# The recurrent layer of a three-layer transformer kernel: gates, first convolution tap, exponentials and b_o in another order

## The chip, the cores and the metric

The kernel runs on one core of one Trainium2 chip. The metric is the device time of one execution in microseconds (us), as the median of several executions.

## What is computed

A sequence of 256 tokens with 1024 channels, all in float32, passes two models one after the other. The first has an attention layer and a recurrent layer, each followed by a feed-forward layer with squared ReLU; the second has one layer with two gated feed-forward parts around a mixer of attention and pooling. The change concerns the recurrent layer alone:

```python
def rglru_block(h, w_in, b_in, conv_w, conv_b, w_ga, b_ga, w_gx, b_gx, a_param, w_o, b_o):
    u = jnp.einsum('bsd,de->bse', h, w_in) + b_in
    x_br = u[..., :D_RNN]
    y_br = jax.nn.gelu(u[..., D_RNN:], approximate=True)
    xp = jnp.pad(x_br, ((0, 0), (CONV_WIDTH - 1, 0), (0, 0)))
    xc = conv_b + xp[:, 0:S] * conv_w[0]
    for tap in range(1, CONV_WIDTH):
        xc = xc + xp[:, tap:tap + S] * conv_w[tap]
    xb = xc.reshape(B, S, N_RG_BLOCKS, RG_BLOCK)
    r = jax.nn.sigmoid(einsum('bsnc,nce->bsne', xb, w_ga) + b_ga)
    ig = jax.nn.sigmoid(einsum('bsnc,nce->bsne', xb, w_gx) + b_gx)
    log_a = -RG_C * r * jax.nn.softplus(-a_param)
    a = jnp.exp(log_a)
    mult = jnp.sqrt(-jnp.expm1(2.0 * log_a))
    b_seq = mult * (ig * xc)
    hs = scan of h = a * h + b_seq over the tokens
    return jnp.einsum('bse,ed->bsd', hs * y_br, w_o) + b_o
```

Here S is 256 and D_RNN is 1024, which the kernel keeps as eight blocks of 128 channels (one block fills the 128 partitions); a gate is a product of a block with its own 128 by 128 matrix.

## The kernel before

**Weights.** All weights pass through TensorE in 167 pieces of 1 MB (128 partitions x 2048 values), in one fixed order. SyncE loads piece n into one of six `raw` buffers, and may do so once piece n - 6 has been split. ScalarE (ACT) copies it to `w_hi`, rounded to fp32r (`hi(n)`, line 318), which needs one of three buffers and so waits until piece n - 3 has been used. VectorE (DVE) subtracts that from the raw piece (`lo(n)`, line 586). A product in full precision is then three fp32r matmuls: high by high, high by low, low by high. The activations are split in the same way into `xT_hi` and `xT_lo`. TensorE waits for both halves of a piece in `split(n)`.

**Order.** Each engine runs a program written out by hand, strictly in its order; they meet in semaphores. Whatever stands behind a waiting instruction on an engine waits too.

**The recurrent layer.** Pieces 48 to 55 (N_REC = 48) are the columns of `w_in`, two channel blocks each: 48 to 51 give the x branch, 52 to 55 the y branch. A piece is eight blocks of six matmuls (`u_block`, lines 1206 to 1209) into one PSUM bank. Pieces 56 to 59 (N_RO = 56) are the rows of the output matrix, 24 matmuls of 512 columns each (`d_part`, line 1230); the last two are closed in an order of their own (`closing`), and FM1, the next feed-forward layer, begins with piece 60.

For a pair p of channel blocks (2p and 2p + 1) the steps are these:

- `x_pair(p)` on VectorE (line 894) takes the pair out of PSUM, times the tokens' rms factor.
- The first tap with the bias is done by GpSimd (POOL, line 1133), the other three taps of both blocks by VectorE in `conv(p)` (line 903), each waiting for the one before.
- `gates(n)` on TensorE (lines 1479 and 1480) needs all taps of block n. The gates of pair p are issued inside piece 50 + p, after its blocks 3 and 6.
- `gates(n)` on ACT takes two sigmoids (lines 478 and 481) and a tanh (line 483) of them; `bx(n)` on GpSimd (line 1138) multiplies the input gate into the block.
- When all eight tanhs are done, ACT takes eight exponentials (line 505). GpSimd squares each (line 1152) into one of two buffers `sq`, VectorE turns square and tanh into the argument of the root (line 949), and ACT takes eight square roots (line 509).
- `scan(n)` on VectorE: for blocks 0 to 3 the product with the root (line 916), which GpSimd does for blocks 4 to 7 (line 1156), and the scan (line 920).
- `y_pair(p)` on VectorE (line 909) takes the y branch out of PSUM, ACT applies the gelu (line 488), `mixed(p)` on VectorE multiplies it with the scan (line 926), ACT copies the product to `xT_hi` (line 496), and VectorE forms `xT_lo` (line 929). The output products of piece 56 + p need both halves of pair p.

GpSimd then adds `b_o` to the residual `h`, in two additions of 128 x 1024 (line 1161), as soon as its own b products are done; VectorE waits for them (`h_bo`) before it adds the outputs to `h` in `turn(M1, ...)`. ACT changes its function tables on the way: the trace has an ACT_TABLE_LOAD ahead of the sigmoids, the exponentials, the roots and the gelus, one each.

VectorE's order in this stretch is: split of 50, rms factor, `x_pair(0)`; then for p = 0, 1, 2 the split of piece 51 + p, `conv(p)`, `x_pair(p + 1)`; split of 54, `conv(3)`, `y_pair(0)`, split of 55, the eight operations of line 949, `y_pair(1)`, split of 56, scans 0 and 1, `mixed(0)`, scans 2 to 7, split of 57, `y_pair(2)`, `mixed(1)`, `y_pair(3)`, `mixed(2)`, `mixed(3)`, splits of 58, 59 and 60.

Of the kernel before, what the change touches and what calls it, by code (L numbers as in the profile page):

```python
# [9 lines left out]
ACT = mybir.ActivationFunctionType  # L10
# [84 lines left out]
def build(nc, A, out):  # L95
# [217 lines left out]
    def scalar(e):  # L313
# [171 lines left out]
        def mixed(p):  # L485
            e.wait_ge(y_left, p + 1)
            for n in (2 * p, 2 * p + 1):
                e.activation(xb[:, n, 0:S], xb[:, n, 0:S], ACT.Gelu_apprx_tanh,
                             bias=col("b_in", KB + n)).then_inc(y_done, 1)
            for n in (2 * p, 2 * p + 1):  # L490
# [7 lines left out]
        for m in range(6):  # L498
            hi(N_REC + m + LOOK)
            if m >= 2:  # L500
                gates(2 * m - 4)
                gates(2 * m - 3)
        e.wait_ge(nt_done, KB)
        for n in range(KB):
            e.activation(rr[:, n, :], rr[:, n, :], ACT.Exp, scale=spn[:, n:n + 1]).then_inc(a_done, 1)
        hi(N_REC + 8)
        for n in range(KB):
            e.wait_ge(m_done, n + 1)
            e.activation(nt[:, n, :], nt[:, n, :], ACT.Sqrt).then_inc(mult_done, 1)
        mixed(0)  # L510
        hi(N_REC + 9)
        for p in range(1, 4):
            mixed(p)
        for n in (N_RO + 2, N_RO + 3, N_RO + 4):
            hi(n)
# [67 lines left out]
    def vector(e):  # L583
# [347 lines left out]

        e.wait_ge(ss_done, 4 * L1 + 4)
# [6 lines left out]
        for p in range(3):  # L939
            lo(N_REC + p + 3)  # L940
            conv(p)
            x_pair(p + 1)
        lo(N_REC + 6)
        conv(3)
        y_pair(0)
        lo(N_REC + 7)
        for n in range(KB):
            e.wait_ge(sq_done, n + 1)
            e.scalar_tensor_tensor(out=nt[:, n, :], in0=sq[n % 2], scalar=1.0, in1=nt[:, n, :], op0=ALU.add,  # L949
                                   op1=ALU.mult).then_inc(m_done, 1)  # L950
        y_pair(1)
        lo(N_REC + 8)
        scan(0)
        scan(1)
        mixed(0)
        for n in range(2, KB):
            scan(n)
        lo(N_REC + 9)
        y_pair(2)
        mixed(1)  # L960
        y_pair(3)
        mixed(2)
        mixed(3)
        for n in (N_RO + 2, N_RO + 3, N_RO + 4):
            lo(n)
# [131 lines left out]
    def gpsimd(e):  # L1097
# [32 lines left out]
        def conv(p):  # L1130
            e.wait_ge(x_left, p + 1)
            for n in (2 * p, 2 * p + 1):
                e.tensor_scalar(xc[:, n, :], xb[:, n, 0:S], col("conv_w", n), conv_bias[:, n:n + 1], ALU.mult,
                                ALU.add).then_inc(conv_first, 1)

# [3 lines left out]

        e.wait_ge(conv_pad, 1)  # L1140
        conv(0)
        for p in range(1, 4):
            conv(p)
            bx(2 * p - 2)
            bx(2 * p - 1)
        bx(6)
        bx(7)
        for n in range(KB):
            e.wait_ge(a_done, n + 1)
            if n >= 2:  # L1150
                e.wait_ge(m_done, n - 1)
            e.tensor_tensor(sq[n % 2], rr[:, n, :], rr[:, n, :], ALU.mult).then_inc(sq_done, 1)
# [6 lines left out]
        e.wait_ge(ss_done, 4 * L1 + 4)  # L1159
        for t in range(T):  # L1160
            e.tensor_tensor(h[:, t, :], h[:, t, :], bo, ALU.add).then_inc(h_bo, 1)
# [33 lines left out]
    def tensor(e):  # L1195
# [290 lines left out]
        for m in range(2, 6):  # L1486
            n, dst = N_REC + m, bank[[6, 4, 5, 6][m - 2]]
            if m >= 3:
                e.wait_ge(x_left, m - 2)
            split(n)  # L1490
            for k in range(KB):
                mm = u_block(n, k, dst)
                if k == KB - 1:
                    mm.then_inc(used, 1)
                if k == 3:
                    gates(2 * m - 4)
                if k == 6:
                    gates(2 * m - 3)
# [192 lines left out]
```

## Time and profile before

| | us |
|---|---|
| median of three executions | 1090.6 (1089.65 to 1091.54) |
| the profiled execution | 1087.43 |
| its span, from the first to the last instruction | 1085.6 |
| PE (TensorE matmul) busy in it | 1034.5 |
| PEld (weight load) busy | 951.8 |
| DVE (VectorE) busy | 684.7 |
| ACT (ScalarE) busy | 483.5 |
| POOL (GpSimd) busy | 91.4 |

The mean granted TensorE clock of the span is 0.985 of full speed. All times of a row count from the span's start. A busy PE is not PE at its peak: matmuls are pipelined, each record is longer than the step to the next one. The recurrent layer lies between about 325 and 412 us: piece 48 near 325, the output products from 388.84 on.

### The profile page before, as it was taken

To read this page: it belongs to the slowest core of one execution; us is meant where nothing else is said; L and a number is where in the kernel's file an instruction comes from. 1 tells how busy PE (TensorE), PEld (TensorE's weight loads), DVE (VectorE), ACT (ScalarE), POOL (GpSimd) and SP (SyncE) were. 2 spreads that over 40 slices of the span, in tenths; PEclk is the share of its full clock that TensorE was granted. 3 is DMA by queue.
4 is the path that set the end of the run, shared out by engine and by line. 5 is a ranking of instruction groups with operands and counts; after the bars stand their busy time and mean duration, and the time that the engine had idled before them with its cause. 6 is when DMAs were issued, how large, how long until landed. Compare 5 with 4: busy or idle time off the path is not lost.

```text
span 1085.6 us, 16423 instructions
## 1 busy us (share of the span) xinstructions
PE 1034.5 (95%) x6956; PEld 951.8 (88%) x6956; DVE 684.7 (63%) x835; ACT 483.5 (45%) x592; POOL 91.4 (8%) x88
## 2 busy tenths in 40 slices
PE   6999899999999959999999999999998789999997
PEld 5999799999989949999989999999987679999996
DVE  5577476655568797665565765565678645655565
ACT  5455353434345744434344644443444244344443
POOL 1200000000005621000000100000014300000000
PEclk9999999999999989999999999999999899999999
DMA  9943336555555325655556465645652226565511
GB/s 344 323 161 118 117 114 206 186 194 194 172 178 179 114 81 210 211 198 176 195 191 187 127 214 199 199 163 194 188 193 78 78 78 212 199 195 191 194 40 39
DMA packets 122838, 185.26 MB, mean 171 GB/s; under 512 B 3034, under 2 KB 102542, under 8 KB 122638
## 3 DMA queue, kind: packets, MB, share of 16 engines
q1 hardware_dynamic: 120784, 177.22, 49.8%
q0 software_dynamic: 1808, 6.93, 1.8%
q8 instruction: 55, 0.90, 0.3%
q14 instruction: 17, 0.14, 0.0%
q10 hardware_dynamic: 174, 0.08, 0.0%
HBM read 183.14 MB, written 1.07 MB: 170 GB/s over the span
## 4 chain that ended last, share of the span: by engine, by line
PE 79%; DVE 5%; issue 2%; ACT 2%; DMA 1%; POOL 0%; DVEq 0%; ACTq 0%; POOLq 0%
PE bank L1230 30%; PE bank L1206 15%; PE bank L1208 15%; PE bank L1209 15%; DVE w_lo L586 1%; PE bank L1256 1%; PE bank L1371 1%; ACT w_hi L318 1%; DMA work<-in_mats 1%; DVE work L926 0%; DVE z_lo L716 0%; PE bank L1480 0%; PE bank L1479 0%; DVE work L990 0%; DVE work L949 0%
## 5 line engine op out<-in xcount | busy, mean ns | idle before, releaser
L586 DVE TENSOR_TENSOR w_lo<-raw,w_hi 128x2048 fp32r<-128x2048 f32 x167 | 383.3, 2300 | 191.9 <-ACT w_hi L318 191.9
L1206 PE MATMUL bank<-xT_hi,w_hi 128*128 128x256 f32 x1552 | 445.3, 287 | 0.0
L1208 PE MATMUL bank<-xT_lo,w_hi 128*128 128x256 f32 x1552 | 439.7, 283 | 0.0
L1209 PE MATMUL bank<-xT_hi,w_lo 128*128 128x256 f32 x1552 | 439.6, 283 | 0.0
L318 ACT ACTIVATE w_hi<-raw 128x2048 fp32r<-128x2048 f32 x167 | 317.7, 1908 | 103.1 <-PE bank L1230 88.3
L1206 PEld LDWEIGHTS bank<-xT_hi,w_hi 128*128 128x128 f32 x1552 | 297.9, 192 | 3.7 <-issue 0.2
L1208 PEld LDWEIGHTS bank<-xT_lo,w_hi 128*128 128x128 f32 x1552 | 298.1, 192 | 2.5 <-issue 0.2
L1209 PEld LDWEIGHTS bank<-xT_hi,w_lo 128*128 128x128 f32 x1552 | 298.0, 192 | 0.0
L1230 PE MATMUL bank<-w_hi,z_hi 128*128 128x512 f32 x432 | 138.6, 392 | 0.3 <-issue 0.3
L1230 PE MATMUL bank<-w_lo,z_hi 128*128 128x512 f32 x432 | 137.6, 390 | 0.0
L1230 PE MATMUL bank<-w_hi,z_lo 128*128 128x512 f32 x432 | 137.4, 390 | 0.0
L1230 PEld LDWEIGHTS bank<-w_hi,z_lo 128*128 128x128 f32 x432 | 81.1, 188 | 17.2
L1230 PEld LDWEIGHTS bank<-w_lo,z_hi 128*128 128x128 f32 x432 | 81.1, 188 | 17.1
L1230 PEld LDWEIGHTS bank<-w_hi,z_hi 128*128 128x128 f32 x432 | 78.0, 189 | 13.8 <-issue 0.7
L356 ACT ACTIVATE z_hi<-work 128x512 fp32r<-128x512 f32 x32 | 20.3, 633 | 143.9 <-DVE work L651 143.9
L1100 POOL TENSOR_TENSOR rstd<-var,minus_half 128x2 f32<-128x2 f32 x7 | 18.7, 2670 | 724.0 <-DVE var L606 724.0
L1230 PE MATMUL bank<-w_hi,xT_hi 128*128 128x512 f32 x128 | 49.3, 435 | 24.7 <-DVE xT_lo L929 11.3
L348 ACT ACTIVATE work<-work 128x512 f32<-128x512 f32 x22 | 13.9, 633 | 97.0 <-DVE work L639 97.0
L1230 PEld LDWEIGHTS bank<-w_hi,xT_hi 128*128 128x128 f32 x128 | 24.8, 202 | 32.0 <-DVE xT_lo L929 11.9
L358 ACT ACTIVATE z_hi<-work 128x512 fp32r<-128x512 f32 x22 | 13.9, 632 | 82.2 <-DVE work L662 82.2
L665 DVE TENSOR_TENSOR z_lo<-work,z_hi 128x512 fp32r<-128x512 f32 x54 | 37.4, 693 | 18.7 <-ACT z_hi L358 15.3
L651 DVE SCALAR_TENSOR_TENSOR work<-bank,rms 128x512 f32<-128x512 f32 x32 | 22.1, 691 | 39.5 <-PE bank L1209 39.3
(182 smaller groups left out, 816.7 us busy)
## 6 DMA issues: line engine op xcount, KB each, us to landing
raw<-in_w SPq DMA_DIRECT2D x64, 1024.0 KB, 5.4
raw<-in_f_gate SPq DMA_DIRECT2D x22, 1024.0 KB, 5.4
raw<-in_f_up SPq DMA_DIRECT2D x22, 1024.0 KB, 5.3
raw<-in_f_down SPq DMA_DIRECT2D x22, 1024.0 KB, 5.0
raw<-in_w_in SPq DMA_DIRECT2D x13, 1024.0 KB, 5.5
raw<-in_w_qkv SPq DMA_DIRECT2D x12, 1024.0 KB, 9.4
raw<-in_w_o SPq DMA_DIRECT2D x4, 1024.0 KB, 7.4
raw<-in_rec_w_o SPq DMA_DIRECT2D x4, 1024.0 KB, 5.6
```

The lines of the kernel that those rows point to most:

```text
L318: e.activation(w_hi[n % RING], raw[n % RAW], ACT.Copy).then_inc(hi_done, 1)
L348: e.activation(tmp[0], tmp[0], ACT.Silu).then_inc(z_s, 1)
L356: e.activation(z_hi[:, s, :], tmp[0], ACT.Square).then_inc(zhi_done, 1)
L358: e.activation(z_hi[:, s, :], tmp[2], ACT.Copy).then_inc(zhi_done, 1)
L586: e.tensor_tensor(w_lo[n % RING], raw[n % RAW], r32(w_hi[n % RING]), ALU.subtract).then_inc(lo_done, 1)
L651: e.scalar_tensor_tensor(out=pair(t), in0=pair(src), scalar=0.0, in1=rms_pair(), op0=ALU.max, op1=ALU.mult).then_inc(z_t, 1)
L665: e.tensor_tensor(z_lo[:, s, :], z, r32(z_hi[:, s, :]), ALU.subtract).then_inc(zlo_done, 1)
L1100: e.tensor_tensor(rstd, var, minus_half, ALU.pow).then_inc(rstd_done, 1)
L1206: e.matmul(o, whi[:, k, cut], xT_hi[:, k, :], start=(k == 0 and b == 0), stop=False, skip_group_check=True)
L1208: e.matmul(o, whi[:, k, cut], xT_lo[:, k, :], start=False, stop=False, skip_group_check=True)
L1209: last = e.matmul(o, wlo[:, k, cut], xT_hi[:, k, :], start=False, stop=(k == KB - 1), skip_group_check=True)
L1230: mm = e.matmul(acc[t][half], x, w[:, kk, half * 512:(half + 1) * 512], start=(first and kk == 0 and x is xhi and w is whi), stop=(last an ...
```

## The change

It is a change of order in the programs of four engines, with the same products on TensorE.

- **TensorE:** gates 0 to 3 are issued inside piece 50 (after its blocks 1, 2, 4 and 6), gates 4 and 5 inside piece 51 and 6 and 7 inside piece 52 (after blocks 3 and 5 of each); piece 53 has none.
- **ACT:** takes over the first tap with its bias (`first_taps`, an Identity with a scale and a bias per partition). The exponentials come in two groups of four (`decays`), the first behind `first_taps(2)` and ahead of the high copy of piece 53, the second behind the last gates. Gelus are a function of their own, ahead of the copies of `mixed`. The high copies of pieces 55 to 57 stand elsewhere.
- **VectorE:** the operations of line 949 come in two groups (`mults`), the first after the split of piece 53 and ahead of `x_pair(3)`. The split of 55 stands behind scans 0 and 1, that of 56 behind all scans; `mixed(0)` comes after the scans and `y_pair(2)`; the split of 57 follows `mixed(3)`.
- **GpSimd:** no first taps; squares in two groups; the additions of `b_o` wait for the tenth count of `mix_lo`, that is until the low parts of `mixed(2)` are done.

```diff
--- before.py
+++ after.py
@@ -482,11 +482,25 @@
             e.wait_ge(r_done, n + 1)
             e.activation(nt[:, n, :], rr[:, n, :], ACT.Tanh, scale=spp[:, n:n + 1]).then_inc(nt_done, 1)
 
-        def mixed(p):
+        def first_taps(p):
+            e.wait_ge(conv_pad, 1)
+            e.wait_ge(x_left, p + 1)
+            for n in (2 * p, 2 * p + 1):
+                e.activation(xc[:, n, :], xb[:, n, 0:S], ACT.Identity, bias=conv_bias[:, n:n + 1],
+                             scale=col("conv_w", n)).then_inc(conv_first, 1)
+
+        def decays(n0):
+            for n in range(n0, n0 + 4):
+                e.wait_ge(nt_done, n + 1)
+                e.activation(rr[:, n, :], rr[:, n, :], ACT.Exp, scale=spn[:, n:n + 1]).then_inc(a_done, 1)
+
+        def gelus(p):
             e.wait_ge(y_left, p + 1)
             for n in (2 * p, 2 * p + 1):
                 e.activation(xb[:, n, 0:S], xb[:, n, 0:S], ACT.Gelu_apprx_tanh,
                              bias=col("b_in", KB + n)).then_inc(y_done, 1)
+
+        def mixed(p):
             for n in (2 * p, 2 * p + 1):
                 e.wait_ge(o_done, n + 1)
                 if n < KB - 1:
@@ -495,24 +509,42 @@
                     e.wait_ge(used, N_REC + 8)
                 e.activation(xT_hi[:, n, :], xc[:, n, :], ACT.Copy).then_inc(mix_hi, 1)
 
-        for m in range(6):
-            hi(N_REC + m + LOOK)
-            if m >= 2:
-                gates(2 * m - 4)
-                gates(2 * m - 3)
-        e.wait_ge(nt_done, KB)
-        for n in range(KB):
-            e.activation(rr[:, n, :], rr[:, n, :], ACT.Exp, scale=spn[:, n:n + 1]).then_inc(a_done, 1)
-        hi(N_REC + 8)
+        hi(N_REC + 2)
+        hi(N_REC + 3)
+        first_taps(0)
+        hi(N_REC + 4)
+        gates(0)
+        first_taps(1)
+        gates(1)
+        gates(2)
+        gates(3)
+        first_taps(2)
+        decays(0)
+        hi(N_REC + 5)
+        gates(4)
+        first_taps(3)
+        gates(5)
+        hi(N_REC + 6)
+        gates(6)
+        gates(7)
+        decays(4)
+        hi(N_REC + 7)
         for n in range(KB):
             e.wait_ge(m_done, n + 1)
             e.activation(nt[:, n, :], nt[:, n, :], ACT.Sqrt).then_inc(mult_done, 1)
+        hi(N_RO)
+        gelus(0)
+        gelus(1)
         mixed(0)
-        hi(N_REC + 9)
-        for p in range(1, 4):
-            mixed(p)
-        for n in (N_RO + 2, N_RO + 3, N_RO + 4):
-            hi(n)
+        hi(N_RO + 1)
+        gelus(2)
+        mixed(1)
+        mixed(2)
+        gelus(3)
+        mixed(3)
+        hi(N_RO + 2)
+        hi(N_RO + 3)
+        hi(FM1.n0)
 
         turn(M1, N_RO + 3 + LOOK)
         feed_forward(FM1)
@@ -929,6 +961,12 @@
                 e.tensor_tensor(xT_lo[:, n, :], xc[:, n, :], r32(xT_hi[:, n, :]),
                                 ALU.subtract).then_inc(mix_lo, 1)
 
+        def mults(n0):
+            for n in range(n0, n0 + 4):
+                e.wait_ge(sq_done, n + 1)
+                e.scalar_tensor_tensor(out=nt[:, n, :], in0=sq[n % 2], scalar=1.0, in1=nt[:, n, :], op0=ALU.add,
+                                       op1=ALU.mult).then_inc(m_done, 1)
+
         e.wait_ge(ss_done, 4 * L1 + 4)
         e.tensor_scalar(xb[:, :, 0:CONV - 1], bcast(vec("b_in")[:, 0:1], [1, KB], [0, CONV - 1]), -1.0, None,
                         ALU.mult).then_inc(conv_pad, 1)
@@ -936,32 +974,35 @@
         spread(L1)
         e.wait_ge(rms_done, L1 + 1)
         x_pair(0)
-        for p in range(3):
-            lo(N_REC + p + 3)
-            conv(p)
-            x_pair(p + 1)
+        lo(N_REC + 3)
+        conv(0)
+        x_pair(1)
+        conv(1)
+        lo(N_REC + 4)
+        x_pair(2)
+        conv(2)
+        lo(N_REC + 5)
+        mults(0)
+        x_pair(3)
+        conv(3)
         lo(N_REC + 6)
-        conv(3)
         y_pair(0)
-        lo(N_REC + 7)
-        for n in range(KB):
-            e.wait_ge(sq_done, n + 1)
-            e.scalar_tensor_tensor(out=nt[:, n, :], in0=sq[n % 2], scalar=1.0, in1=nt[:, n, :], op0=ALU.add,
-                                   op1=ALU.mult).then_inc(m_done, 1)
-        y_pair(1)
-        lo(N_REC + 8)
+        mults(4)
         scan(0)
         scan(1)
-        mixed(0)
-        for n in range(2, KB):
+        lo(N_REC + 7)
+        scan(2)
+        scan(3)
+        y_pair(1)
+        for n in range(4, KB):
             scan(n)
-        lo(N_REC + 9)
+        lo(N_RO)
         y_pair(2)
-        mixed(1)
+        for p in range(3):
+            mixed(p)
         y_pair(3)
-        mixed(2)
         mixed(3)
-        for n in (N_RO + 2, N_RO + 3, N_RO + 4):
+        for n in (N_RO + 1, N_RO + 2, N_RO + 3, FM1.n0):
             lo(n)
 
         e.wait_ge(h_bo, 2)
@@ -1127,29 +1168,21 @@
         rstds(L1)
         e.dma_start(bo, row_bcast(A["b_o"], D)).then_inc(in_b_o, 16)
 
-        def conv(p):
-            e.wait_ge(x_left, p + 1)
-            for n in (2 * p, 2 * p + 1):
-                e.tensor_scalar(xc[:, n, :], xb[:, n, 0:S], col("conv_w", n), conv_bias[:, n:n + 1], ALU.mult,
-                                ALU.add).then_inc(conv_first, 1)
-
         def bx(n):
             e.wait_ge(ig_done, n + 1)
             e.tensor_tensor(xc[:, n, :], xc[:, n, :], ig[n % 2], ALU.mult).then_inc(bx_done, 1)
 
-        e.wait_ge(conv_pad, 1)
-        conv(0)
-        for p in range(1, 4):
-            conv(p)
-            bx(2 * p - 2)
-            bx(2 * p - 1)
-        bx(6)
-        bx(7)
-        for n in range(KB):
-            e.wait_ge(a_done, n + 1)
-            if n >= 2:
-                e.wait_ge(m_done, n - 1)
-            e.tensor_tensor(sq[n % 2], rr[:, n, :], rr[:, n, :], ALU.mult).then_inc(sq_done, 1)
+        def squares(n0):
+            for n in range(n0, n0 + 4):
+                e.wait_ge(a_done, n + 1)
+                if n >= 2:
+                    e.wait_ge(m_done, n - 1)
+                e.tensor_tensor(sq[n % 2], rr[:, n, :], rr[:, n, :], ALU.mult).then_inc(sq_done, 1)
+
+        for n0 in (0, 4):
+            for n in range(n0, n0 + 4):
+                bx(n)
+            squares(n0)
         for n in range(KB // 2, KB):
             e.wait_ge(mult_done, n + 1)
             e.wait_ge(bx_done, n + 1)
@@ -1157,6 +1190,8 @@
         e.wait_ge(in_b_o, 16)
         e.wait_ge(turned, KB * L1 + KB)
         e.wait_ge(ss_done, 4 * L1 + 4)
+
+        e.wait_ge(mix_lo, 4 + 6)
         for t in range(T):
             e.tensor_tensor(h[:, t, :], h[:, t, :], bo, ALU.add).then_inc(h_bo, 1)
         rstds(M1)
@@ -1483,19 +1518,11 @@
         u_piece(N_REC + 1, bank[5], {3: lambda: spread(L1)})
         e.wait_ge(in_gate_a, 16)
         e.wait_ge(in_gate_x, 16)
-        for m in range(2, 6):
-            n, dst = N_REC + m, bank[[6, 4, 5, 6][m - 2]]
+        for m, dst, beside in ((2, bank[6], {1: 0, 2: 1, 4: 2, 6: 3}), (3, bank[4], {3: 4, 5: 5}),
+                               (4, bank[5], {3: 6, 5: 7}), (5, bank[6], {})):
             if m >= 3:
                 e.wait_ge(x_left, m - 2)
-            split(n)
-            for k in range(KB):
-                mm = u_block(n, k, dst)
-                if k == KB - 1:
-                    mm.then_inc(used, 1)
-                if k == 3:
-                    gates(2 * m - 4)
-                if k == 6:
-                    gates(2 * m - 3)
+            u_piece(N_REC + m, dst, {k: lambda n=n: gates(n) for k, n in beside.items()})
         e.wait_ge(rms_done, L1 + 1)
         u_piece(N_REC + 6, bank[7])
         e.wait_ge(x_left, 4)
```

## Rows read from the trace of the kernel before

**Rows 1.** The page, busy time, share of the span and instructions of each engine.
```profile
PE 1034.5 (95%) x6956; PEld 951.8 (88%) x6956; DVE 684.7 (63%) x835; ACT 483.5 (45%) x592; POOL 91.4 (8%) x88
```

**Rows 2.** Waits, 325 to 425 us: us in total, times, longest.
```profile
PE bank L1230 <- DVE xT_lo L929: 11.3, 2, 10.3
```

**Rows 3.** Windows of PE: stretch, length, busy (instructions), granted clock, DMA share, GB/s.
```profile
382.00:384.00 2.00, 0.00 (x0) 0.76 0.71 289
...
388.00:390.00 2.00, 1.16 (x3) 0.50 0.00 0
...
392.00:394.00 2.00, 2.00 (x8) 0.68 0.00 0
```

**Rows 4.** Timeline of PE: start, us, line, operation, tiles; idle before and releaser in brackets.
```profile
339.89 0.59 PE L1479 MATMUL bank<-work,gate_w 128*128 128x256 f32 x2
...
340.56 0.47 PE L1206 MATMUL bank<-xT_hi,w_hi 128*128 128x256 f32 x1
...
342.05 0.28 PE L1209 MATMUL bank<-xT_hi,w_lo 128*128 128x256 f32 x1
...
342.77 0.28 PE L1209 MATMUL bank<-xT_hi,w_lo 128*128 128x256 f32 x1
...
388.84 1.22 PE L1230 MATMUL bank<-w_hi,xT_hi 128*128 128x512 f32 x2 [10.34 <-DVE xT_lo L929]
...
393.27 0.65 PE L1230 MATMUL bank<-w_hi,xT_lo 128*128 128x512 f32 x2
...
397.63 0.73 PE L1230 MATMUL bank<-w_hi,xT_hi 128*128 128x512 f32 x2 [0.96 <-DVE xT_lo L929]
...
402.77 0.61 PE L1230 MATMUL bank<-w_hi,xT_lo 128*128 128x512 f32 x2
405.28 0.47 PE L1230 MATMUL bank<-w_hi,xT_hi 128*128 128x512 f32 x1 [1.90 <-DVE w_lo L586]
```

**Rows 5.** Timeline of DVE, 325 to 425 us.
```profile
335.40 2.28 DVE L586 TENSOR_TENSOR w_lo<-raw,w_hi 128x2048 fp32r<-128x2048 f32 x1
338.15 2.99 DVE L903 SCALAR_TENSOR_TENSOR work<-work,cols 128x256 f32<-128x256 f32 x6 [0.47 <-POOL work L1133]
341.05 0.68 DVE L894 TENSOR_TENSOR work<-bank,rms 128x512 f32<-128x512 f32 x1
...
344.40 3.82 DVE L903 SCALAR_TENSOR_TENSOR work<-work,cols 128x256 f32<-128x256 f32 x6 [0.47 <-POOL work L1133]
...
370.11 1.15 DVE L949 SCALAR_TENSOR_TENSOR work<-work 128x256 f32<-128x256 f32 x2 [4.89 <-POOL work L1152]
...
378.97 0.94 DVE L916 TENSOR_TENSOR work<-work 128x256 f32<-128x256 f32 x1
...
380.97 0.88 DVE L916 TENSOR_TENSOR work<-work 128x256 f32<-128x256 f32 x1
...
382.89 4.98 DVE L926 TENSOR_TENSOR work<-work 128x256 f32<-128x256 f32 x2
...
390.19 3.02 DVE L920 TENSOR_TENSOR_SCAN work<-work 128x256 f32<-128x256 f32 x5
...
395.92 0.75 DVE L926 TENSOR_TENSOR work<-work 128x256 f32<-128x256 f32 x2
```

**Rows 6.** Timeline of POOL, 325 to 425 us.
```profile
345.12 1.78 POOL L1138 TENSOR_TENSOR work<-work 128x256 f32<-128x256 f32 x2
...
382.39 5.20 POOL L1161 TENSOR_TENSOR h<-h,work 128x1024 f32<-128x1024 f32 x2
```

**Rows 7.** Timeline of ACT, 325 to 425 us.
```profile
343.96 0.47 ACT L478 ACTIVATE work<-bank,cols 128x256 f32<-128x256 f32 x1 [1.77 <-PE bank L1480]
...
345.09 1.91 ACT L318 ACTIVATE w_hi<-raw 128x2048 fp32r<-128x2048 f32 x1
...
367.05 0.51 ACT L483 ACTIVATE work<-work,extra 128x256 f32<-128x256 f32 x1
...
368.87 3.31 ACT L505 ACTIVATE work<-work,extra 128x256 f32<-128x256 f32 x8
```


## The prediction

> **What bounds the kernel now.** I read the shares of the page first: TensorE is busy for 95% of the span [rows 1], so a change to the recurrence can win only where TensorE stands still there. The waits of the stretch from 325 to 425 us say where: its output products (L1230) wait 11.3 us in two stops for the low parts of the mixed activations [rows 2]. The windows add the clock: TensorE stops near 378.5, the granted clock falls near 383 to 0.50 (the 1.2 GHz level) and is back at 1.00 (2.4 GHz) only near 393.3, after it resumed: 0.76, 0.50 and 0.68 are the means of three windows [rows 3]. In the PE timeline the same gap is the idle time of 10.34 us ahead of 388.84; pieces 56 and 57 are the first two output pieces, and piece 58 begins at 405.28 after a wait of 1.90 for low weights [rows 4]. From 405.28 on PE is fed and everything later simply moves with it. So one number decides: **when piece 58 can begin, against 405.28**.
>
> The DVE timeline says what is late. VectorE runs a weight split (2.28), six taps (0.50 apiece) and an exit from PSUM (0.68) in turn, waits 4.89 us ahead of 370.11 for the tail (exponentials, squares, roots), and then pays for two multiplications of L926 4.98 us, where the same two take 0.75 at 395.92 [rows 5]. Beside them stand GpSimd's two additions of b_o, 5.20 us from 382.39 [rows 6]. They alternate: a VectorE operation with two SBUF inputs does not run while a GpSimd one does. That costs 4.2 us on the path to 388.84, and it is what the change moves.
>
> **The change, part by part, on the profiled execution's clock.** Units: a block of six u matmuls is 0.72 (342.05 to 342.77); the two gates of a channel take 0.67 (339.89 to 340.56) and 0.17 more at the re-entry (17 matmuls of 0.12 from 340.56 would end in 342.60, not 342.77), 0.85 in all; 24 output matmuls at full clock are 5.6 (397.63 to 402.77 is 22 of them) [rows 4]. Piece 50 begins at 339.89 - 4 x 0.72 = 337.0. A channel's three gate activations on ACT are 1.13 (343.96 to 345.09), an exponential 0.40 and so, I take it, a gelu, a high copy of weights 1.9, and a table switch 1.39: the exponentials at 368.87 follow the tanh at 367.05 by 1.82 where 0.43 is usual [rows 7].
>
> *First tap on ACT.* Removed: eight GpSimd operations and VectorE's wait of 0.47 for them in each of four rounds [rows 5]. Added: eight ACT operations. No Identity is in the trace; between an exponential (0.40) and the tanh (0.51) [rows 7] I take 0.42, 0.85 a pair. But they now queue on ACT behind gates. The split of 51 begins at 335.4 and ends at 337.6; conv(0) needs no GpSimd and has its channels at 339.15 and 340.6.
>
> *Four gates in piece 50.* TensorE reaches gates(0) at 338.45 and waits to 339.2, gates(1) at once, gates(2) after first_taps(1), which sits behind gates(0) on ACT (free at 341.6): taps from 342.2, channel 2 at 343.75, a wait of 0.7. The piece ends at 337.0 + 8 x 0.72 + 4 x 0.85 + 1.5 of waits = 347.7.
>
> *Exponentials in the middle.* x_pair(2) needs piece 50, so 347.9 to 348.6; first_taps(2) to 349.4; switch to Exp, four exponentials to 352.4; only then the high copy of piece 53, done at 354.3. VectorE, finished with conv(2) at 352.9 (bx and squares each take 0.4 from it, as 3.82 with two of them against 2.99 without for six taps show [rows 5, 6]), waits for it, splits to 356.6, does mults(0) in about 2.5 (1.15 a pair, and turns with GpSimd's squares [rows 5]) and takes x_pair(3) only at 359.0 although piece 51 ended at 355.4. conv(3) gives channel 6 at 361.8: gates(6), reached at 358.35 in piece 52, stop TensorE for **3.5 us**. Piece 52 ends at 366.4. Two more table switches than before (Exp and back to Sigmoid) are in this: the first lies on the path to the copy of 53, the second is covered, since ACT is ready at 356.7 and x_pair(3) is not.
>
> *Tail.* gates(7) leave ACT at 366.3, switch, exponentials 4 to 7 from 367.8, squares and mults(4) to 371.8; meanwhile the copy of 55, a switch, and the first root ends at 373.0. A product with its scan costs VectorE 2.0 beside GpSimd (378.97 to 380.97) and 1.0 alone. In the new order come: scans 0 and 1, the second beside GpSimd, 2.9; the split of 55 with a GpSimd operation ahead of it 2.9; scans 2 and 3 beside the last two 3.4; y 0.6; four scans 2.4; the split of 56 2.2; y 0.6; mixed(0), two products, two copies on ACT and the low parts, 1.7 [rows 5]: 373.0 + 16.7 = **389.7** for the first output product, 0.9 later than 388.84, though 4.2 of collision have left this part. Piece 55 itself waited 0.8 for its split and ends near 384.7, so the idle gap is 5 us, not 10.3; piece 56 runs to about 395.4, or 397 if the clock fell.
>
> *b_o during the outputs.* Behind mixed(0), ACT does the high copy of 57 and gelus(2) first (3 us), so mixed(1) and mixed(2) end at 394.7. That is the tenth count of the low parts, and GpSimd starts its 5.2 us. VectorE's y_pair(3) reads PSUM; no row has such an operation beside a GpSimd one. Free of it, it costs 0; blocked, GpSimd would at most start 0.5 later. I take 0. Gelus(3) leave at 396.2, and now the two multiplications of mixed(3) meet the additions exactly as mixed(0) does in the trace: the second product ends near 400.3 instead of 396.6, the low parts at 401.2. **Queued behind them on VectorE is the split of piece 57**, which before stood ahead of y_pair(2): 401.2 + 2.3 = 403.5. TensorE, done with piece 56 at 395 to 397, waits 6 to 8 us for it; before, piece 57 began at 397.63.
>
> *Sum.* Piece 58 begins at 403.5 + 5.6 = 409.1 plus what a fallen clock costs. Bounds: 0, and the 2.1 us of the trace (ten matmuls from 388.84 to 393.27 in 4.43 instead of 2.3 [rows 4]) after a longer gap. I take 1.1. So 410.2 - 405.3 = **+4.9 us**. The profiled execution took 1087.4 with 1085.6 of span, 3.2 below the median of 1090.6; on the median that is 1095.5. DMAs move little: SP's loads hang on the splits, of which 56 comes sooner and 57 8 us later, and the pieces they bring lie beyond 60 and are needed some 20 us on; I cost them at nothing.
>
> **A rule against the trace.** A switch of the activation table costs 1.39 us here [rows 7]. The Trainium skill (ScalarE: Activation LUTs, What ACT_TABLE_LOAD costs) states about 2.66 us for every switch. By it the copy of 53 would be 1.3 later and the sum about +6.2 us instead of +4.9, as in rival 5. The trace does not show its drain of 1.38.
>
> **Rivals.** (1) *The b_o additions miss mixed(3).* If VectorE's two products slip in before or between them, the split of 57 ends at 399.3, piece 57 at 404.9: -0.4 us, up to +1.5 with a slow clock. For it: VectorE has only a few operations there. Against it: gelus(3) need y_pair(3) first, so the products come 1 us after GpSimd has started, and the same pair collided in full in the trace. Time 1091.2.
> (2) *The middle is faster than I walk it.* If ACT reaches the copy of 53 or VectorE x_pair(3) 3 us sooner, TensorE's 3.5 us stall goes, all below moves by 3 and leaves +1.9: 1092.5. The walk has many steps of 0.1 to 0.3 uncertain, but ACT's order is fixed.
> (3) *Faster.* GpSimd no longer blocks VectorE at all in these places: bx, squares and b products (some 2.5 us before 389.7) and the additions (3.9) cost nothing, and the gap is too short for the clock to fall. Then +4.9 - 2.5 - 3.9 - 1.1 = -2.6 us, 1088.0. It decides at the duration of L926 in mixed(3): under 0.5 us each. Against it stand the 0.9 to 1.1 us operations at 378.97 and the 4.98 us at 382.89 [rows 5].
> (4) *Identity is not in the loaded table.* Then first_taps between gates bring up to five further switches of 1.39, some 4 of the 7 us on the path: +9 us, 1099.5. The Trainium skill (ScalarE: Activation LUTs, Table sets) says every set holds it.
> (5) *A switch in mid-stream holds ACT twice as long as at 368.87.* Then the Exp switch ahead of the copy of 53 costs 1.4 more, all below moves, and the sum is +6.3: 1096.9. Against it: the one switch measured between two dependent ACT steps cost 1.39. The page named above gives such a price, and its section on table sets asks to batch calls by set, which this change undoes.
>
> **How the numbers follow.** Forecast as walked, with or without the clock's cost: 0.58, +3.5 to +7. Rival 1: 0.14. Rival 2: 0.10. Rival 3: 0.10. Rival 4: 0.03. Rival 5: 0.05. A measurement of this kernel tells about 0.2% (2.2 us) from no change. Faster by more: rival 3, 0.10. Within it: most of rivals 1 and 2, 0.21. Slower: 0.69. The range goes from 1090.0, which takes in rivals 1, 2 and 5, to 1099.0, a walk that is late by 2 us with the full cost of the clock; rivals 3 and 4 and the tails lie outside.
>
> **What would show it.** Right: L926 at twice 2.5 us in mixed(3) beside GpSimd's additions at 395 to 400; the split of 57 only near 401; waits of PE L1230 for it of 6 us or more and a low granted clock there; PE waiting about 3.5 us at L1479 for a tap; two ACT table loads more; first output product at 389 to 390. Wrong: L926 at 0.4 us everywhere, an output product before 387, or no wait at gates(6).

## The result, and the profile after

| | before | after |
|---|---|---|
| median of six executions, us | 1090.12 | 1096.06 |
| lowest and highest | 1087.23, 1091.55 | 1093.53, 1098.97 |
| profiled execution, span | 1087.43, 1085.6 | 1096.55, 1094.8 |

The ratio of after to before is 1.0062 with a 95% interval of 1.0045 to 1.0080: **5.9 us slower on the medians**, 6.8 by the ratio, where 4.9 were forecast.

The profiled pair lies 9.1 us apart. The copy of the rms factor marks each layer, and its starts sort this out. VectorE's timeline has them for the recurrent layer and the next one, before:

```profile
334.34 0.42 DVE L633 COPY rms<-bank 128x256 f32<-128x256 f32 x1 [0.38 <-PE bank L1293]
...
427.38 0.42 DVE L633 COPY rms<-bank 128x256 f32<-128x256 f32 x1 [0.45 <-PE bank L1293]
```

and after:

```profile
333.16 0.42 DVE L665 COPY rms<-bank 128x256 f32<-128x256 f32 x1 [0.38 <-PE bank L1328]
...
433.67 0.42 DVE L665 COPY rms<-bank 128x256 f32<-128x256 f32 x1 [0.45 <-PE bank L1328]
```

From copy to copy the recurrent layer takes 93.0 us before and 100.5 after, 7.5 us more. The second model's mixer, which the change does not touch, takes 107.4 us before (798.13 to 905.55) and 110.3 after (804.39 to 914.67); over the traces of all thirteen kernels of this page it is 107.2 to 108.1 in five and 109.4 to 111.1 in eight, whatever the kernel, so that part is a difference between executions. Times of after below are as its rows have them; **add 1.2 us to compare them with rows of before or with the forecast's clock**.

The line numbers have moved: output products L1265 (were L1230), gates L1514 (L1479), taps L935 (L903), x exits L926 (L894), products of `mixed` L958 (L926), low parts L961 (L929), b_o L1196 (L1161), splits L618 (L586), exponentials L495 (L505). First the waits of PE in 325 to 425 us, which answer to [rows 2]; columns as there.

```profile
PE bank L1265 <- DVE w_lo L618: 6.1, 1, 6.1
PE bank L1514 <- DVE work L935: 5.3, 4, 4.1
PE bank L1265 <- DVE xT_lo L961: 4.3, 1, 4.3
```

Before there was one large stop of 10.3 us and two of 1 to 2 us, 13.2 us in all. Now there are three large ones: 4.1 us for a tap (the longest of four, 5.3 together), 4.3 for low activations, 6.1 for the low half of a weight piece, 15.7 in all. The timeline of PE puts them in order (gates(6), first output product, piece 57, piece 58), as [rows 4] did.

```profile
361.63 1.22 PE L1514 MATMUL bank<-work,gate_w 128*128 128x256 f32 x2 [4.08 <-DVE work L935]
...
366.06 1.06 PE L1514 MATMUL bank<-work,gate_w 128*128 128x256 f32 x2
...
391.13 1.23 PE L1265 MATMUL bank<-w_hi,xT_hi 128*128 128x512 f32 x2 [4.27 <-DVE xT_lo L961]
...
404.49 1.19 PE L1265 MATMUL bank<-w_hi,xT_hi 128*128 128x512 f32 x2 [6.12 <-DVE w_lo L618]
...
411.68 0.39 PE L1265 MATMUL bank<-w_hi,xT_hi 128*128 128x512 f32 x1
```

Piece 58 begins at 411.68, in before's clock 412.9 against 405.28. And here is what a stop costs beyond itself, the windows of PE (stretch, length, busy, granted clock, DMA share, GB/s):

```profile
361.00:363.00 2.00, 1.37 (x3) 0.50 0.00 0
...
365.00:367.00 2.00, 2.00 (x9) 0.50 0.07 17
367.00:369.00 2.00, 2.00 (x17) 0.99 0.93 255
...
404.00:406.00 2.00, 1.51 (x4) 0.50 0.23 65
406.00:408.00 2.00, 2.00 (x6) 0.50 1.01 325
```

The clock was at its lower level (0.50, 1.2 GHz) from the stall at gates(6) on, through the gates and the blocks between them, and again when piece 57 began. VectorE's timeline shows the two places where its queue made these stops:

```profile
353.57 2.29 DVE L618 TENSOR_TENSOR w_lo<-raw,w_hi 128x2048 fp32r<-128x2048 f32 x1 [2.06 <-ACT w_hi L318]
355.78 0.75 DVE L967 SCALAR_TENSOR_TENSOR work<-work 128x256 f32<-128x256 f32 x2
...
358.64 0.68 DVE L926 TENSOR_TENSOR work<-bank,rms 128x512 f32<-128x512 f32 x1
...
375.44 0.42 DVE L948 TENSOR_TENSOR work<-work 128x256 f32<-128x256 f32 x1 [1.23 <-ACT work L534]
...
395.13 0.77 DVE L961 TENSOR_TENSOR xT_lo<-work,xT_hi 128x256 fp32r<-128x256 f32 x2
395.81 0.68 DVE L941 TENSOR_TENSOR work<-bank,rms 128x512 f32<-128x512 f32 x1
397.07 4.16 DVE L958 TENSOR_TENSOR work<-work 128x256 f32<-128x256 f32 x2 [0.58 <-ACT work L500]
...
402.06 6.69 DVE L618 TENSOR_TENSOR w_lo<-raw,w_hi 128x2048 fp32r<-128x2048 f32 x3
```

At 353.57 VectorE has waited 2.06 us for the high copy of piece 53, and x_pair(3) (L926) stands behind that split and the operations of L967. At 397.07 the two products of mixed(3) take 4.16 us, and the split of 57 is the first of the three at 402.06. The low parts of mixed(2) at 395.13 are what GpSimd's additions wait for. GpSimd's timeline there:

```profile
396.07 4.88 POOL L1196 TENSOR_TENSOR h<-h,work 128x1024 f32<-128x1024 f32 x2 [13.87 <-DVE xT_lo L961]
```

and that of ACT:

```profile
347.62 1.10 ACT L489 ACTIVATE work<-work,extra,cols 128x256 f32<-128x256 f32 x2 [0.26 <-DVE work L926]
348.73 1.28 ACT L495 ACT_TABLE_LOAD   x1
350.03 1.71 ACT L495 ACTIVATE work<-work,extra 128x256 f32<-128x256 f32 x4
351.64 1.90 ACT L318 ACTIVATE w_hi<-raw 128x2048 fp32r<-128x2048 f32 x1
353.56 1.28 ACT L478 ACT_TABLE_LOAD   x1
```

GpSimd's additions of b_o run from 396.07 to 400.95, over the products at 397.07. On ACT the first taps of pair 2, a table load, four exponentials, the copy of piece 53 and another load follow each other without a gap.

### The profile page after: what moved, and what is told of

It is laid out like the page before. It is cut to its first block, busy times and chain, and to the rows that moved or that the text cites. A ratio compares the mean times of both kernels' runs of the same rounds, so it can differ in the third digit from the quotient of the medians.

```text
span 1094.8 us, 16429 instructions
## 1 busy us (share of the span) xinstructions
PE 1039.9 (95%) x6956; PEld 955.0 (87%) x6956; DVE 682.2 (62%) x835; ACT 490.2 (45%) x602; POOL 77.5 (7%) x80
## 4 chain that ended last, share of the span: by engine, by line
PE 77%; DVE 6%; ACT 3%; issue 2%; DMA 1%; POOL 0%; DVEq 0%; ACTq 0%; POOLq 0%
PE bank L1265 31%; PE bank L1241 14%; PE bank L1244 14%; PE bank L1243 14%; DVE w_lo L618 2%; ACT w_hi L318 1%; PE bank L1291 1%; PE bank L1406 1%; DMA work<-in_mats 1%; DVE work L958 0%; DVE z_lo L748 0%; PE bank L1514 0%; DVE work L935 0%; DVE work L756 0%; PE bank L1394 0%
## 5 line engine op out<-in xcount | busy, mean ns | idle before, releaser
L618 DVE TENSOR_TENSOR w_lo<-raw,w_hi 128x2048 fp32r<-128x2048 f32 x167 | 382.6, 2296 | 198.4 <-ACT w_hi L318 198.4
L1265 PE MATMUL bank<-w_hi,z_hi 128*128 128x512 f32 x432 | 138.6, 392 | 0.3 <-issue 0.3
L1265 PE MATMUL bank<-w_lo,z_hi 128*128 128x512 f32 x432 | 137.6, 390 | 0.0
L1265 PE MATMUL bank<-w_hi,z_lo 128*128 128x512 f32 x432 | 137.5, 390 | 0.0
L1265 PEld LDWEIGHTS bank<-w_hi,z_lo 128*128 128x128 f32 x432 | 81.1, 188 | 17.2
L1265 PEld LDWEIGHTS bank<-w_lo,z_hi 128*128 128x128 f32 x432 | 81.1, 188 | 17.1
L1265 PEld LDWEIGHTS bank<-w_hi,z_hi 128*128 128x128 f32 x432 | 78.0, 189 | 13.8 <-issue 0.6
L1265 PE MATMUL bank<-w_hi,xT_hi 128*128 128x512 f32 x128 | 50.8, 448 | 21.9 <-DVE w_lo L618 9.3
L1265 PEld LDWEIGHTS bank<-w_hi,xT_hi 128*128 128x128 f32 x128 | 26.0, 212 | 29.1 <-issue 10.1
L1265 PE MATMUL bank<-w_lo,xT_hi 128*128 128x512 f32 x128 | 47.7, 423 | 0.0
```

Of the source, the lines that this page charges most:

```text
L618: e.tensor_tensor(w_lo[n % RING], raw[n % RAW], r32(w_hi[n % RING]), ALU.subtract).then_inc(lo_done, 1)
L1265: mm = e.matmul(acc[t][half], x, w[:, kk, half * 512:(half + 1) * 512], start=(first and kk == 0 and x is xhi and w is whi), stop=(last an ...
```

## The experiments

All were measured in five rounds against the kernel before, in 5 to 12 executions each. "Against after" gives two differences to the kernel after: that of the medians (to 1096.06), and that of the ratios, times 1090 us. The second allows for the kernel before, whose medians in these rounds were 1089.68, 1089.37 and 1089.08 us and not 1090.12. "Layer" is the recurrent layer from rms copy to rms copy in the one profiled execution. It leaves out the rest of the program, but still varies: three kernels that are the same up to the first output product (after, e1, e2) reach it 58.0, 56.9 and 58.3 us behind the copy.

| run | what | median us | ratio to before, 95% interval | against after, us | layer, us |
|---|---|---|---|---|---|
| before | | 1090.12 | | | 93.0 |
| after | | 1096.06 | 1.0062 (1.0045 to 1.0080) | | 100.5 |
| e1_no_adds | after, b_o left out | 1091.91 | 1.0016 (1.0003 to 1.0030) | -4.2, -5.0 | 94.5 |
| e2_early57 | after, split of 57 earlier | 1093.96 | 1.0033 (1.0021 to 1.0046) | -2.1, -3.2 | 98.8 |
| e3_adds_back | after, b_o where it was | 1095.68 | 1.0057 (1.0043 to 1.0072) | -0.4, -0.5 | 100.3 |
| e4_tail | after, exponentials all late | 1091.92 | 1.0024 (1.0013 to 1.0035) | -4.1, -4.1 | 97.0 |
| e11_middle_reordered | after, middle in another order | 1093.84 | 1.0034 (1.0020 to 1.0048) | -2.2, -3.1 | 96.7 |
| e9_before_wait | before, b_o deferred | 1089.55 | 1.0000 (0.9989 to 1.0010) | | 93.0 |
| e13_before_taps_on_act | before, first taps on ACT | 1089.47 | 1.0002 (0.9990 to 1.0014) | | 93.1 |
| e5_before_dve_adds | before, b_o on VectorE | 1085.61 | 0.9953 (0.9938 to 0.9969) | | 88.8 |
| e6_early58 | e5, split of 58 earlier | 1082.17 | 0.9936 (0.9917 to 0.9955) | | 86.8 |
| e8_hybrid | new order of all parts | 1083.68 | 0.9949 (0.9935 to 0.9962) | | 87.8 |
| e10_hybrid_y_first | e8, y_pair first | 1080.96 | 0.9925 (0.9910 to 0.9940) | | 84.2 |

### The outputs: b_o and the split of piece 57

e1, GpSimd's additions and VectorE's wait for them left out:

```diff
-        e.wait_ge(h_bo, 2)
...
-        e.wait_ge(mix_lo, 4 + 6)
-        for t in range(T):
-            e.tensor_tensor(h[:, t, :], h[:, t, :], bo, ALU.add).then_inc(h_bo, 1)
```

> The changed kernel without GpSimd's two additions of b_o (the output lacks b_o). My theory: they hold VectorE's products of mixed(3) for 3.4 us (397.07 to 401.2), and behind them the split of piece 57, for which TensorE waits 6.1 us. Without them the split ends near 401.0, the gap shrinks to 2.8 us, and the time falls by 3.4 us, or by 5.0 if the clock then stays up: 1091 to 1092.7. Rival, that TensorE's late arrival from the middle is the whole loss: within 1 us of the changed kernel, 1096.

Measured 1091.91, 4.2 us faster, within the 1091 to 1092.7 expected. The products of mixed(3) take 0.83 instead of 4.16, and TensorE waits 1.80 for the split of 57 instead of 6.12. In this trace the timeline of DVE says the first:

```profile
396.85 0.83 DVE L958 TENSOR_TENSOR work<-work 128x256 f32<-128x256 f32 x2 [0.58 <-ACT work L500]
...
398.51 6.69 DVE L618 TENSOR_TENSOR w_lo<-raw,w_hi 128x2048 fp32r<-128x2048 f32 x3
```

that of PE the second:

```profile
400.94 0.70 PE L1257 MATMUL bank<-w_hi,xT_hi 128*128 128x512 f32 x2 [1.80 <-DVE w_lo L618]
```

and in the windows of PE the granted clock was still 1.00 when piece 57 began:

```profile
400.00:402.00 2.00, 1.06 (x5) 1.00 0.04 10
```

e2, the split of 57 ahead of `y_pair(3)` on VectorE:

```diff
+        lo(N_RO + 1)
         y_pair(3)
         mixed(3)
-        for n in (N_RO + 1, N_RO + 2, N_RO + 3, FM1.n0):
+        for n in (N_RO + 2, N_RO + 3, FM1.n0):
```

> The changed kernel with the split of piece 57 ahead of y_pair(3). My theory: piece 57 follows piece 56 almost at once; the additions of b_o then delay mixed(3) and the split of 58 to about 405.6, which piece 58 waits for; it begins 6 us sooner than at 411.7: 1090. Rival, that the products of mixed(3) set the end whatever stands behind them: no more than 2 us gained, 1094.

Measured 1093.96, the rival's number, and in the main its mechanism. Piece 57 does follow at once; piece 58 then waits 4.00 us and begins at 408.58, 3.1 us sooner than at 411.68, not 6. I had expected its split to be done near 405.6. The timelines show two causes for the rest. The split of 57 started 0.25 us ahead of GpSimd's additions (396.45 and 396.70), which beside it took 6.88 us, and so the products of mixed(3) ended near 403.8 instead of 401.2. And the split of 58 waits 1.38 more for ACT, whose high copy of 58 is also queued behind mixed(3). DVE:

```profile
396.45 2.28 DVE L618 TENSOR_TENSOR w_lo<-raw,w_hi 128x2048 fp32r<-128x2048 f32 x1
398.65 0.69 DVE L941 TENSOR_TENSOR work<-bank,rms 128x512 f32<-128x512 f32 x1
399.91 3.94 DVE L958 TENSOR_TENSOR work<-work 128x256 f32<-128x256 f32 x2 [0.58 <-ACT work L500]
403.78 0.99 DVE L961 TENSOR_TENSOR xT_lo<-work,xT_hi 128x256 fp32r<-128x256 f32 x2
406.14 6.70 DVE L618 TENSOR_TENSOR w_lo<-raw,w_hi 128x2048 fp32r<-128x2048 f32 x3 [1.38 <-ACT w_hi L318]
```

ACT:

```profile
403.89 0.42 ACT L510 ACTIVATE xT_hi<-work 128x256 fp32r<-128x256 f32 x1 [2.12 <-DVE work L958]
404.22 5.50 ACT L318 ACTIVATE w_hi<-raw 128x2048 fp32r<-128x2048 f32 x3
```

GpSimd:

```profile
396.70 6.88 POOL L1197 TENSOR_TENSOR h<-h,work 128x1024 f32<-128x1024 f32 x2 [13.87 <-DVE xT_lo L961]
```

PE:

```profile
408.58 0.47 PE L1266 MATMUL bank<-w_hi,xT_hi 128*128 128x512 f32 x1 [4.00 <-DVE w_lo L618]
```

e3, only the wait of the additions dropped (the line `e.wait_ge(mix_lo, 4 + 6)`):

> The changed kernel without GpSimd's wait for the tenth count of the low parts: b_o is added right behind the b products, near 382, as before the change. My theory: the 4 us of blocked VectorE move from mixed(3) to the scans and y_pair(1) ahead of mixed(0); the first output product comes 4 us later, the split of 57 at about the same time, and the time stays: 1095 to 1098. Rival, that the place of b_o was what made the changed kernel slow: at least 3 us faster, under 1093.

Measured 1095.68, not to be told from after. The collision moved to a product and a scan of the recurrence, 2.56 and 2.76 us instead of 0.4 and 0.7, and TensorE's stop for the low activations is 8.51 us instead of 4.27, the one for the split 2.15 instead of 6.12. The timeline of DVE:

```profile
382.56 2.56 DVE L948 TENSOR_TENSOR work<-work 128x256 f32<-128x256 f32 x1
385.15 2.76 DVE L952 TENSOR_TENSOR_SCAN work<-work 128x256 f32<-128x256 f32 x1
```

and of PE:

```profile
395.25 1.22 PE L1263 MATMUL bank<-w_hi,xT_hi 128*128 128x512 f32 x2 [8.51 <-DVE xT_lo L961]
...
405.28 0.70 PE L1263 MATMUL bank<-w_hi,xT_hi 128*128 128x512 f32 x2 [2.15 <-DVE w_lo L618]
```

e9, the same wait added to the kernel before and nothing else:

> The kernel before with one part of the change alone, GpSimd's wait for the tenth count of the low parts ahead of the additions of b_o. My theory: mixed(0) is 4.2 us sooner, but the second product and the low parts of mixed(3) meet the additions and delay the split of 58 to about 404.4; piece 58 begins within 1 us of 405.3: 1088.5 to 1090. Rival, that the deferral is good by itself and only the other parts cost: 1086.

Measured 1089.55, ratio 1.0000. What mixed(0) gained (first output product at 384.68 instead of 388.84) was lost again: piece 58 waited 4.53 us for its split instead of 1.90 and began at 403.75, 1.5 us sooner than before, and its first part ran at the lower clock (0.50 from 404 to 406). So the deferral is neutral by itself in either order; the additions block VectorE for 3 to 4.3 us wherever they meet it (here the products and the low parts of mixed(3) took 2.98 and 2.92 instead of 0.82 each), and VectorE is the late engine in both places.

### The middle: exponentials, mults and the copy of piece 53

e4, all exponentials after the last gates, squares and mults likewise in one group:

```diff
         def decays(n0):
-            for n in range(n0, n0 + 4):
+            for n in range(n0, KB):
...
-        decays(0)
         hi(N_REC + 5)
...
-        decays(4)
+        decays(0)
         hi(N_REC + 7)
...
         def mults(n0):
-            for n in range(n0, n0 + 4):
+            for n in range(n0, KB):
...
-        mults(0)
         x_pair(3)
...
-        mults(4)
+        mults(0)
         scan(0)
...
```

> The changed kernel with all eight exponentials, squares and operations of line 949 after the last gates, as before the change (two table switches fewer); gates, first taps and b_o as changed. My theory: the copy of piece 53 comes 3 us sooner, x_pair(3) follows piece 51 at once, gates(6) do not wait 4.1 us and the clock does not fall there; the longer tail gives back about half: 3.4 us faster, 1092.7. Rival, that splitting the exponentials pays for its stall: same or slower than the changed kernel, 1096 or more.

Measured 1091.92, 4.1 us faster (3.4 expected). The stop at gates(6) is 0.17 us and x_pair(3) begins at 355.53. The waits for taps are 1.4 us in all four gates together, against 5.3. What is left to the kernel before, 4.0 us in the layer, stands in the tail and the outputs: TensorE waits 2.86 us for the split of 55, which VectorE does behind scans 0 and 1, 2.37 for the first output product and 6.04 for the split of 57.

e11 keeps both groups and both added table switches, and moves only the queue places:

```diff
+        hi(N_REC + 5)
         decays(0)
-        hi(N_REC + 5)
...
-        mults(0)
         x_pair(3)
         conv(3)
+        mults(0)
```

> The changed kernel with the high copy of piece 53 ahead of decays(0) on ACT, and x_pair(3) and conv(3) ahead of mults(0) on VectorE; both groups of four exponentials and both added table switches stay. My theory: the stall of 4.1 us at gates(6) falls below 1 us and the clock stays up; the first root comes 4.3 us sooner than at 375.0: 1091.8, as fast as e4, so that the two queue places and not the switches cost the time. Rival, that the added table switches are what delays the middle: 1095 or more.

Measured 1093.84, between the expectation and the rival. Its first half holds: gates(6) wait 0.64, the roots begin at 370.62 instead of 374.99, the first output product at 386.77 instead of 391.13 and piece 57 at 400.16 instead of 404.49, all 4.3 to 4.4 us sooner. The lower clock then lasted past 404, and piece 58 began 3.5 sooner, at 408.15. The two queue places are thus shown to make the stall. Whether they are the whole loss of the middle is less sure. In the traces they are: the layer is as short as in e4 (96.7 and 97.0 us), and the 3 us by which the profiled execution of e11 is longer lie outside it. The medians gained 2.2 and those of e4 4.1, with overlapping intervals. So two groups with two more switches cost the same as one group: within 0.3 us in this pair of traces, which can differ by about 1 us for no reason of the kernel's, and within 2 us on the medians.

The timeline of PE, that of ACT and PE's windows:

```profile
358.47 0.70 PE L1514 MATMUL bank<-work,gate_w 128*128 128x256 f32 x2 [0.64 <-DVE work L935]
...
400.16 1.19 PE L1265 MATMUL bank<-w_hi,xT_hi 128*128 128x512 f32 x2 [5.38 <-DVE w_lo L618]
```

```profile
370.62 2.57 ACT L534 ACTIVATE work<-work 128x256 f32<-128x256 f32 x8
```

```profile
404.00:406.00 2.00, 2.00 (x7) 0.67 1.10 358
```

e13, the first tap on ACT alone, in the kernel before (`first_taps(m - 1)` behind `hi(N_REC + m + LOOK)`, no taps on GpSimd):

> The kernel before with the first tap on ACT alone. VectorE no longer waits 0.47 us for GpSimd in each round. My theory: TensorE does not wait there and the tail hangs on the last gates, which TensorE issues at the same time as before: no change, 1089.4 within 1 us. Rival, that the taps on ACT bring something by themselves: 1087 or less.

Measured 1089.47, no change. VectorE's rounds are shorter, and the tail begins no sooner, since the gates are issued at the same time.

Together: of the 6 to 7 us, e4 and e11 put 3 to 4 on the stall in the middle. The deferral of b_o by itself is worth nothing (e3, e9). The rest belongs to the order of the outputs, where splits stand behind other work on VectorE (the waits left in e4, and e2 for the split of 57). No run joins e2 and e11, so that the two parts add up is argued from the traces and not shown.

### A version that beats both

e5, the kernel before with b_o added by VectorE behind the split of 55 (L950), where it was idle:

```diff
         lo(N_REC + 7)
+        e.wait_ge(in_b_o, 16)
+        e.wait_ge(turned, KB * L1 + KB)
+        for t in range(T):
+            e.tensor_tensor(h[:, t, :], h[:, t, :], bo, ALU.add).then_inc(h_bo, 1)
...
```

> The kernel before, with b_o added by VectorE itself in its idle time ahead of 370.11 (two operations of some 1.1 us in 4.9 us) and not by GpSimd. My theory: the collision of 4.2 us in mixed(0) is gone and all behind it moves by 4.2: 1086. Rival, that the low parts of mixed(0) wait for something else as well (ACT, the clock): within 1 us of before, 1089 to 1090.

Measured 1085.61, 4.1 us faster than the 1089.68 of before in the same rounds. Both additions take 2.89 us at 365.48, in the gap; the products of mixed(0) take 0.73. The timeline of DVE, and of PE:

```profile
365.48 2.89 DVE L950 TENSOR_TENSOR h<-h,work 128x1024 f32<-128x1024 f32 x2
...
383.25 0.73 DVE L926 TENSOR_TENSOR work<-work 128x256 f32<-128x256 f32 x2
```

```profile
384.94 1.22 PE L1229 MATMUL bank<-w_hi,xT_hi 128*128 128x512 f32 x2 [6.08 <-DVE xT_lo L929]
```

e5 and e1 are the two orders without the collision. The order after is still the slower one, by 6.3 us on the medians and 5.7 in the layer. So the collision, dear as it is in both kernels (5.1 and 5.0 us by the ratios), is not what sets them apart.

e6, in addition the high copy of 58 behind that of 57 on ACT, its split ahead of mixed(3) on VectorE:

> Run e5 with the high copy of piece 58 ahead of gelus(1) on ACT and its split ahead of mixed(3) on VectorE. In e5 TensorE waits 1.9 us for that split, and VectorE 1.4 us for the copy. My theory: piece 58 then follows piece 57 directly: 1.9 us faster than e5, 1083.7. Rival, that mixed(3) behind the split is now late for piece 59: no gain.

Measured 1082.17, 3.4 us below e5 on the medians, with intervals that overlap; by the ratios it is 1.9 and in the layer 2.0, as expected. In its trace PE waits for no split in this stretch any more.

e8, gates and first taps as changed, everything else in a new order (VectorE's part; ACT follows it):

```diff
+        mixed(0)
         lo(N_RO)
+        scan(2)
+        scan(3)
+        y_pair(1)
+        mixed(1)
+        lo(N_RO + 1)
...
```

> Gates and first taps as changed, exponentials, squares and line 949 in the tail as in e4, b_o added by VectorE in two idle places, and the outputs interleaved: mixed(0) behind scans 0 and 1, then for each pair a split, two scans, y_pair and mixed. My theory: the gates gain 4 us at the front of the tail, nothing collides, the gap ahead of the outputs shrinks to about 1 us, the clock stays up, and piece 58 begins near 395.5: 1080. Rival, that ACT and VectorE then run late within the outputs: 1084 or more.

Measured 1083.68, 3.7 us above the expectation. The gap ahead of the outputs is 1.38 us and piece 58 begins at 395.73, both as meant, but PE waits 5.4 us in four places for splits: VectorE is then the engine that paces the outputs. I had counted its work and left out its waits for the gelus, 0.58 us in each of three rounds. The last stop, for the split of 59, was followed by the lower clock; the timeline of PE and its window:

```profile
402.02 0.47 PE L1269 MATMUL bank<-w_hi,xT_hi 128*128 128x512 f32 x1 [1.93 <-DVE w_lo L617]
```

```profile
404.00:406.00 2.00, 2.00 (x7) 0.50 1.05 361
```

e10 puts each `y_pair` ahead of its two scans:

> Run e8 with each y_pair ahead of the two scans of its round. In e8 VectorE is busy from 371.7 to 401.8 but for three waits of 0.58 us for the gelus, and TensorE waits 5.4 us in four places for splits. My theory: the gelus hide behind the scans, the splits of 57, 58 and 59 come 0.6, 1.2 and 1.7 us sooner, and so does the end: 1082. Rival, that the waits for splits have another cause than VectorE's queue: no change, 1083.7.

Measured 1080.96, **8.1 us under the 1089.08 of before in its own rounds** and 2.7 below e8, where 1.7 were expected. PE's waits for splits fall to 3.3 us (the waits of PE, then its windows), and the clock never left its upper level in the outputs:

```profile
PE bank L1269 <- DVE w_lo L617: 3.3, 3, 1.4
```

```profile
388.00:390.00 2.00, 1.67 (x7) 1.00 0.27 56
```

Its interval and that of e6 overlap, so which of the two is faster is open; both beat the kernels before and after.

## Why the prediction was right

**What bounds.** It named one number, the start of piece 58: 410.2 forecast, 412.9 measured in that clock, so +7.6 in the layer where +4.9 was forecast; the medians say +5.9. That the median came out within 0.6 us of the 1095.5 forecast is partly luck: in the trace the walk is 2.7 us short, and the terms below say where.

**First tap on ACT.** Forecast neutral, and e13 shows it. A pair took 1.09 and not 0.85 us on ACT.

**Four gates in piece 50.** Waits of 0.57 and 0.53 us at gates(0) and gates(2), forecast 0.75 and 0.7.

**Exponentials in the middle.** The chain was right link by link: the copy of 53 behind the exponentials, its split, mults(0), x_pair(3) at 358.64 + 1.2 = 359.8 (forecast 359.0), the stop at gates(6) 4.08 us (forecast 3.5). The term that was mis-sized is what follows: the forecast let the gates and blocks behind the stall run at full clock. From gates(6) to gates(7) it was 4.43 us (361.63 to 366.06), where 2.3 were forecast, at a granted clock of 0.50. gates(7) left ACT at 370.0 in before's clock, not at 366.3. This cost too varies: behind the same stop the same stretch took 4.43 us in e2, 3.81 in e1 and 3.85 in e3, and 2.40 at full clock in e4 and e11.

**Tail.** VectorE's 16.7 us from the first root to the first output product were 15.7 (375.44 to 391.13), so the product came at 392.3, 2.6 late.

**b_o during the outputs.** This part was right term by term. Products of mixed(3) 4.16 us, behind them the split of 57 at 402.06, TensorE waiting 6.12: all as written. From the first output product to piece 57 it was 13.4 us, forecast 13.8. y_pair(3), which reads PSUM, took 0.68 with GpSimd's addition starting inside it, and 0.69 in e2, where the additions ran from 396.70 all the way past it: the choice of 0 was right.

**The clock's cost in piece 57.** Taken as 1.1, bounds 0 and 2.1. Piece 57 took 7.19 us (404.49 to 411.68) instead of 5.6: 1.6.

**The rivals.** (1) is refuted by the 4.16 us; its 404.9 is also misnamed, since 399.3 + 5.6 is where piece 58 would begin, not piece 57. (2) came the other way, the middle was slower. (3) is refuted by the same row. (4): the trace has no load at the first taps; they follow the gates at 340.45 in after's ACT timeline at once. (5) is refuted as well. It is the price of about 2.66 us for a switch that the Trainium skill states (ScalarE: Activation LUTs, What ACT_TABLE_LOAD costs). Here the exponentials at 350.03 start 2.41 after the taps at 347.62, which take 0.99 of that to issue; 1.42 is the switch. The measurement decides against the total of the Trainium skill.

## What to carry to other kernels

An operation that is taken off one critical place should be asked what it meets in the next: here the additions cost VectorE 3 to 4.3 us wherever GpSimd made them beside it, and the path nothing when VectorE made them in its own idle time. On an engine with a fixed order, list what stands behind a delayed step (the split of 57, the copy of 53, then the copy of 58) rather than the step itself. And price a TensorE stall of some 4 us with the slow clock after it, a third to half as much again in this case (1.4 to 2.0 us).

## What the runs showed of the hardware that was not expected

A stop of 4.08 us, in a stretch that was otherwise full, was enough to bring the granted clock down to 0.50, and the work from 361.63 to 367 ran at it, some 5.4 us; after the stop of 4.27 us ahead of 391.13 the windows show 0.50 from 392 to 394 and 0.91 in the next two us, while after the same stop in e1 they show 0.50 from 390 to 396 and then 0.94. Shorter stops went both ways. The one of 1.80 us in e1 and one of 1.92 us in e5 left the clock at 1.00; after the 1.93 us in e8 it was 0.50 from 404 to 406, and after the 2.86 us in e4 0.50 from 380 to 382.

VectorE adds 128 x 1024 values twice in 2.89 us in the idle stretch. GpSimd's two additions took 4.88 to 5.31 us with VectorE's operations waiting between them, and 6.88 in e2, where a split of VectorE's ran among them.
